# Forming the reciprocal of a softmax row sum on GpSimd instead of VectorE, in a two-layer encoder trunk

## The reference

```python
mod = (c_act @ w_ada[l] + b_ada[l])[:, None, :]
sh_a, sc_a, g_a, sh_m, sc_m, g_m = jnp.split(mod, 6, axis=-1)
h = x * (1.0 + sc_a) + sh_a
proj = h @ w_in[l]
y_a = dilated_mixture(...)   # 4 heads, three window patterns with a relative bias
y_b = mla_attention(...)     # 4 heads, low-rank q and kv, 96 wide
y_c = axial_gqa(...)         # 8 query heads over 2 key heads, 64 wide
y = concat(y_a, y_b, y_c) @ w_o[l]
x = layer_norm(ALPHA * x + (1.0 + g_a) * y, ln1_g[l], ln1_b[l])
h = x * (1.0 + sc_m) + sh_m
y = jnp.square(jax.nn.relu(h @ w1[l])) @ w2[l]
x = layer_norm(ALPHA * x + (1.0 + g_m) * y, ln2_g[l], ln2_b[l])
```

## Time and profile before

| | |
|---|---|
| runs | 1500.44, 1501.14, 1495.86 us, median 1500.44 |
| profiled execution | 1502.46 us, span 1500.70, mean granted clock 0.963 |
| TensorE busy | 1348.9 us (90%) |
| VectorE busy | 1054.1 us (70%), 1830 instructions |
| ScalarE busy | 599.4 us (40%) |
| GpSimd busy | 294.4 us (20%), 312 instructions |
| normalise, line 453 | 128 instructions, 96.5 us busy, 238.7 us idle before them |

### The profile page before, as it was taken

The page is one execution under the profiler, slowest core; times in us unless marked ns, Lnnn a source line. Parts: engine busy times, 40 slices in busy tenths (PEclk is TensorE's granted clock), DMA queues, the critical chain, the costliest instruction groups (busy, mean ns, idle before and its releaser), DMA issues.

```text
span 1500.7 us, 23220 instructions
## 1 busy us (share of the span) xinstructions
PE 1348.9 (90%) x6728; PEld 1126.7 (75%) x6728; DVE 1054.1 (70%) x1830; ACT 599.4 (40%) x1216; POOL 294.4 (20%) x312
## 2 busy tenths in 40 slices
PE   5998987799899999999959898869989999999992
PEld 2897866687688887878759877758778878788772
DVE  6667699877688465565765878979675865565578
ACT  0356387661532122222144647868153222222121
POOL 0031075220125000000410404723010700000024
PEclk9999999899999999999979998989989999999996
DMA  8854700004233333334236462010423333233421
GB/s 298 291 180 159 223 8 14 26 15 151 82 126 125 120 119 119 95 118 151 71 131 202 154 205 69 1 38 1 141 81 123 127 119 119 91 126 121 146 98 56
DMA packets 92131, 174.14 MB, mean 116 GB/s; under 512 B 8124, under 2 KB 18748, under 8 KB 92024
## 3 DMA queue, kind: packets, MB, share of 16 engines
q1 hardware_dynamic: 91496, 170.79, 34.8%
q10 hardware_dynamic: 528, 2.10, 0.4%
HBM read 168.66 MB, written 4.19 MB: 115 GB/s over the span
## 4 chain that ended last, share of the span: by engine, by line
PE 58%; DVE 15%; DMA 10%; issue 9%; ACT 5%; POOL 2%; SPq 1%; DVEq 0%; ACTq 0%; POOLq 0%
PE bank L1303 18%; PE bank L1305 18%; PE bank L1304 18%; DMA slab_raw<-in_w_in 5%; DVE ada_sum L820 2%; DMA ada_w<-in_w_ada 2%; DMA slab_raw<-in_w 1%; PE bank L1332 1%; DVE pt_lo L1060 1%; DVE smax L1047 1%; PE bank L1470 1%; DVE X L1088 1%; DVE tmp L1085 1%; DVE k_lo L1018 1%; DMA band<-bias_rows 1%
## 5 line engine op out<-in xcount | busy, mean ns | idle before, releaser
L1303 PE MATMUL bank<-hT_hi,slab_hi 128*128 128x512 f32 x576 | 224.5, 390 | 2.8 <-ACT kB L640 2.8
L1305 PE MATMUL bank<-hT_hi,slab_lo 128*128 128x512 f32 x576 | 224.2, 389 | 0.0
L1304 PE MATMUL bank<-hT_lo,slab_hi 128*128 128x512 f32 x576 | 224.1, 389 | 0.0
L1303 PE MATMUL bank<-slab_hi,h_hi 128*128 128x512 f32 x512 | 203.8, 398 | 5.6 <-ACT mod_a L791 5.6
L1304 PE MATMUL bank<-slab_lo,h_hi 128*128 128x512 f32 x512 | 202.3, 395 | 0.0
L1305 PE MATMUL bank<-slab_hi,h_lo 128*128 128x512 f32 x512 | 202.1, 395 | 0.0
L1140 DVE TENSOR_TENSOR slab_lo<-slab_raw,slab_hi 128x512 fp32r<-128x512 f32 x240 | 178.3, 798 | 22.5 <-ACT slab_hi L774 15.6
L820 DVE SCALAR_TENSOR_TENSOR ada_sum<-ada_w,c_col,ada_sum 128x512 f32<-128x512 f32 x196 | 153.3, 782 | 24.3 <-DMA ada_w<-in_w_ada 20.2
L1303 PE MATMUL bank<-slab_hi,hT_hi 128*128 128x384 f32 (+3 forms) x448 | 152.8, 341 | 14.1 <-ACT tmp L535 5.4
L1305 PE MATMUL bank<-slab_hi,hT_lo 128*128 128x384 f32 (+3 forms) x448 | 151.5, 338 | 0.0
L1304 PE MATMUL bank<-slab_lo,hT_hi 128*128 128x384 f32 (+3 forms) x448 | 151.4, 338 | 0.0
(11 more groups left out here) (197 smaller groups left out, 2605.5 us busy)
## 6 DMA issues: line engine op xcount, KB each, us to landing
slab_raw<-in_w SPq DMA_DIRECT2D x256, 256.0 KB, 2.7
ada_w<-in_w_ada SPq DMA_DIRECT2D x56, 1024.0 KB, 5.9
slab_raw<-in_w_in SPq DMA_DIRECT2D x48, 192.0 KB, 4.8
slab_raw<-in_w_o SPq DMA_DIRECT2D x32, 256.0 KB, 2.7
slab_raw<-in_w_in SPq DMA_DIRECT2D x16, 256.0 KB, 3.4
band<-bias_rows SPq DMA_DIRECT2D x8, 448.0 KB, 3.2
slab_raw<-in_w_in SPq DMA_DIRECT2D x16, 144.0 KB, 4.4
X<-in_x SPq DMA_DIRECT2D x1, 2048.0 KB, 10.3
```

Source lines behind the costliest of these rows:

```text
L1303: pe.matmul(dst, a_hi, w_hi, start=first, stop=False)
L1304: pe.matmul(dst, a_hi, w_lo, start=False, stop=False)
L1305: return pe.matmul(dst, a_lo, w_hi, start=False, stop=last)
```

## The change

The reciprocal instruction on VectorE is gone, with its two waits and the semaphore `summed`. GpSimd waits for the exponential (`exped`) instead, forms the row sum to the power minus one with a `tensor_tensor` on one column against a constant column `mone`, waits for that result on its own step semaphore, and multiplies as before. `mone` is set once at the start.

```diff
+        mone = keep("mone", [P, 1])
...
+            pool.memset(mone[:, :], -1.0).then_inc(setup_pool, 1)
-            pool.wait_ge(setup_pool, 3)
+            pool.wait_ge(setup_pool, 4)
...
-            pool.wait_ge(setup_pool, 4)
-            PER = 6 * TT + TT + 2 * TT + 2 * TT + 2 + 4
+            pool.wait_ge(setup_pool, 5)
+            PER = UNITS + 6 * TT + TT + 2 * TT + 2 * TT + 2 + 4
...
                 for u in range(UNITS):
-                    wait_apart(pool, summed, l * UNITS + u + 1)
+                    wait_apart(pool, exped, l * UNITS + u + 1)
                     p = prob[:, u % 4, :]
+                    step(pool.tensor_tensor(smax[:, u % 4, 2:3], smax[:, u % 4, 1:2], mone[:, :], ALU.pow))
+                    wait_apart(pool, pool_step, l * PER + steps[0])
                     pool.tensor_scalar(p, p, smax[:, u % 4, 2:3], 1.0, ALU.mult, ALU.mult).then_inc(normed, 1)
...
-                    u = s - 1
-                    if 0 <= u < UNITS:
-                        dve.wait_ge(exped, l * UNITS + u + 1)
-                        if u >= 4:
-                            dve.wait_ge(normed, l * UNITS + u - 3)
-                        dve.reciprocal(smax[:, u % 4, 2:3], smax[:, u % 4, 1:2]).then_inc(summed, 1)
...
-            pe.wait_ge(setup_pool, 4)
+            pe.wait_ge(setup_pool, 5)
```

More of the change, by code:

```diff
@@ L248, in trunk @@
             sem, ("k_hi_done", "head_hi", "head_ready", "v_hi_done", "v_ready"))
-        scored, maxed, exped, summed, normed, transposed, pt_hi_done, pt_ready, pv_done, y_hi_done, y_ready = map(
-            sem, ("scored", "maxed", "exped", "summed", "normed", "transposed", "pt_hi_done", "pt_ready",
+        scored, maxed, exped, normed, transposed, pt_hi_done, pt_ready, pv_done, y_hi_done, y_ready = map(
+            sem, ("scored", "maxed", "exped", "normed", "transposed", "pt_hi_done", "pt_ready",
                   "pv_done", "y_hi_done", "y_ready"))
```

## The result

The changed kernel takes 1507.73 us (median of 8 runs, 1504.98 to 1511.29) against 1500.26 of the kernel before (8 runs). Slower was right. The size was not, and the larger part of the miss is a term that the prediction does not have at all.

A forecast was written before the change was run, and what follows sets the result against it. GpSimd was taken to set the pace in units 8 to 23 of each attention stage. Per layer 12.2 + 0.5 - 1.0 - 2.3 = +9.4 us, +18.8 for two, giving 1519.2 us, range 1508 to 1532.

The forecast's parts named there:

- The price of a power: On GpSimd, each one-column power takes 0.55 us plus 0.21 for its wait, 0.76 a unit (0.64 to 0.91).
- The full stretch: Units 8 to 23 of an attention stage, GpSimd full: 16 powers add 12.2 us a layer (10.2 to 14.6).
- the rival of the collisions: Units 8 to 23: powers and VectorE's q, k, v preparations delay each other, 6.3 us more a layer, 1531.8; chance 0.12.
- The start of the stage: First units of an attention stage: the bare lead-in of the normalise grows, +0.5 us a layer (0 to 1).
- The relief and what comes back: After units 8 to 23, backlog returns 1.0 us a layer; fewer reciprocals on VectorE in units 24-31, A, B give 2.3.
- the fourth rival: Heads of A: VectorE no longer waiting for the exponential's sum frees TensorE's stalls, -3.3 us a layer, 1493; chance 0.04.
- The attention stage in all: Both layers' attention stages: +9.4 us each, +18.8 us together.
- all of it arrives at the end: Work behind attention starts from its last head, so the whole +18.8 us shows in the kernel's time.
- the stages behind attention as long as before: Expected sign in the profile: stages after attention keep their length.
- The power as cheap as an add: GpSimd's power costs 0.19 us plus 0.21 wait, so 3.6 us a layer, 1507.6; chance 0.06.
- The clock: TensorE's clock falls to 1.2 GHz; some two units a layer behind the stretch run 1.0 us longer, 1523.2; chance 0.15.
- the bound of 2.3 us after the stretch: Largest backlog return behind units 8 to 23, in us a layer: an exponential's 1.34 us wait, a max and a reciprocal.

The follow-up runs named there:

- the kernel that moves no tile: The changed kernel with the minus one kept in a free column of `mhalf`, so no tile moves: 1515.86 us, ratio 1.0100 to the kernel before.

## Why the prediction was wrong

**The price of a power: right.** 0.55 and 0.21 us, taken from a norm's power and from the extra increment in the wait, were 0.55 and 0.21. The bounds 0.19 and 0.70 for the power and 0.09 for the wait were not needed; the mean was 0.65 in the stretch, with three powers of 1.00 us that began while VectorE prepared a q.

**The full stretch: right.** +12.2 forecast, +11.65 measured. The mean power was 0.1 longer than taken, and the normalise and the multiplying pieces became shorter (808 to 736 and 1394 to 1289 ns). Of the sixteen normalises, seven overlap one of VectorE's preparations of q, k or v before and three after, where six powers do, so collisions moved from the one to the other. This is the argument that was held against the rival of the collisions.

**The start of the stage: right.** +0.5 forecast, +0.7 measured: 0.5 ahead of the first normalise and 0.2 up to the ninth.

**The relief and what comes back: near in sum, misplaced.** -3.3 a layer forecast, -4.1 and -3.9 measured. Units 24 to 31 were to give 1.6 and gave 1.8. B was to give 1.1 and gave nothing (+0.2 by the normalises), though VectorE's reciprocal is gone there. The prediction calls VectorE the engine with least slack in B, but its own row has TensorE busier, 34.96 of 36.00 us against 34.86. That window also begins in A; in one that holds B alone the kernel before has

```profile
297.00:322.00 25.00, 24.78 (x176) 21.91 (x174) 24.02 (x53) 21.74 (x52) 11.04 (x14) 1.00 0.01 2
```

so TensorE was in B at least as full as VectorE, and a lighter VectorE had little to give. A was to give 0.6 and gave 2.5. The row sum of the last unit of a head in A waited for its reciprocal, which stood on VectorE behind the first maximum of the next head, and that waits for the band. This is close to the claim of the fourth rival, that A's stalls come from VectorE's order; the prediction set it aside, with a chance of 0.04 that all of them go. Unit 43 on ScalarE, VectorE and GpSimd, before and after:

```profile
281.01 0.19 ACT L698 ACTIVATION_READ_ACCUMULATOR prob<-prob,smax 128x1 f32 x1
...
283.86 0.69 DVE L1040 CUSTOM_DVE_ANT_0 prob<-bank,band 128x512 f32<-128x512 f32 x1 [1.92 <-DMA band<-bias_rows]
...
284.68 0.16 DVE L1054 RECIPROCAL smax<-smax 128x1 f32<-128x1 f32 x1
...
285.05 0.69 POOL L453 TENSOR_SCALAR prob<-prob,smax 128x512 f32<-128x512 f32 x1 [3.72 <-DVE smax L1054]
```

```profile
289.75 0.19 ACT L702 ACTIVATION_READ_ACCUMULATOR prob<-prob,smax 128x1 f32 x1
...
290.87 0.70 POOL L457 TENSOR_SCALAR prob<-prob,smax 128x512 f32<-128x512 f32 x1 [0.21 <-POOL smax L455]
...
292.58 0.69 DVE L1044 CUSTOM_DVE_ANT_0 prob<-bank,band 128x512 f32<-128x512 f32 x1 [1.98 <-DMA band<-bias_rows]
```

The normalise comes 3.8 us behind the sum before and 0.9 after, and the wait for the band is as long as it was. Units 35 and 39 show the same (3.4 and 3.9 before, 0.9 and 1.0 after). That this wait is what gave A its 2 us was not tested by itself.

**The attention stage in all: right within its own bounds.** 18.8 us forecast for both layers, 16.8 in the profiles, and 15.0 by the time of the kernel that moves no tile; the bounds gave 10.2 to 29.

**The step that failed** is "all of it arrives at the end", with "the stages behind attention as long as before". The delay did arrive. What was taken for unchanged was not: the new tile moved every tile behind it by 32 bytes, and the second MLP product got faster by 4.7 us in layer 0 and 4.8 in layer 1. The prediction read the added line as a memset and never as an allocation, and so put this term at nothing. Without it the forecast of 1519.2 stands against 1515.9, well inside the range; with it the time is 1507.7, just outside.

**The rivals.** The power as cheap as an add would have given the measured time to 0.1 us, 1507.6, and is refuted by its own row (0.55). This is worth keeping in mind: the total alone would have confirmed the wrong mechanism. The collisions on top did not come: the q preparations in the stretch became shorter too, 1011 ns in the mean against 1288. The clock stayed at 2.4 GHz in the new stretch of both layers and for the 16 us behind it (granted clock 1.00). The relief of VectorE was real, but with all that came back behind the stretch it was 4.1 us a layer, not the 11.7 it would have needed.

Two small slips in the prediction's working move nothing but the low bound, by 0.2 us: the bound of 2.3 us after the stretch adds up to 2.2, and TensorE's 1.5 us of work a unit is 1.9 by its own row (29.84 in sixteen units).

## What to carry to other kernels

Ask of each engine how full it is in the stretch that an edit touches, not over the span: a 0.76 us addition was free in 48 units of a stage and cost nearly in full in 16. Divide stages by an instruction that the edit leaves alone. Read an allocation in a diff as a change to every tile behind it, and compare the mean of the same matmuls before and after in the stages the change does not touch. When total and forecast mechanism agree, look for the mechanism's own row before believing it.

## What the runs showed of the hardware

The place of the weights of a split float32 matmul counts: with the h2 tiles at 32 modulo 64 bytes in the partition, two of the three groups of matmuls have a mean of 395 ns, at 0 modulo 64 of 389, and the third 398 and 393. This holds with no exception in thirteen kernels, three at the one place and ten at the other, and is 0.5% of this kernel. Whether other placements than these two are slower, and whether moving operands mind, was not tried.

GpSimd's power on one column with exponent minus one takes 0.55 us where nothing disturbs it, as long as with minus one half. A wait with an increment between it and the instruction leaves 0.21 us behind it on GpSimd, 0.12 more than the 0.09 of the plain one.
